# Three-product fp32r projection tiles for q, k, v and conv in a hybrid decoder layer, with the first 16 K pages loaded up front

## The reference

```
p = rmsnorm(h, norm_w) @ w_in           # 9232 columns: conv q/k/v, z, a, b, q_b, k_b, v_b, two gates
q, k, v = silu(causal_conv(qkv))        # gated delta rule, chunked, 8 heads of 128
o_a = gdn_scan(...)
z = q_b @ k_b * SCALE + bias            # stick-breaking attention on the prompt
# the 8 sampled tokens: the same against 2048 cached keys and values each
kp = cache_k[page_table]; vp = cache_v[page_table]      # 16 pages of 128 rows, 8 heads x 128
z = einsum('bqhd,bkhd->bhqk', q, kp)
m = sigmoid(gate_a) * (o_a @ w_pa) + sigmoid(gate_b) * (o_b @ w_pb)
h = h + m @ w_o;  h = h + (silu(gate) * up) @ w_ffn_out;  y = rmsnorm(h)
```

## Time and profile before

| what | value |
|---|---|
| three runs | 1638.34, 1641.56 (median), 1643.76 us |
| profiled execution | 1639.83 us, its span 1638.1 us |
| mean granted TensorE clock in it | 0.934 of full speed |
| busy | PE 1496.4 us (91%), DVE 751.4, ACT 503.7, POOL 139.4 |

### The profile page before, as it was taken

How to read it: one execution, slowest core, us unless ns; L and a number is a source line. 1 busy time by engine, 2 the same in 40 slices (tenths; PEclk the granted TensorE clock), 3 DMA queues, 4 the chain that set the end, 5 groups by cost and what they waited for, 6 DMA issues and landing times.

```text
span 1638.1 us, 26196 instructions
## 1 busy us (share of the span) xinstructions
PE 1496.4 (91%) x9866; PEld 1303.6 (80%) x9866; DVE 751.4 (46%) x2955; ACT 503.7 (31%) x725; POOL 139.4 (9%) x228
## 2 busy tenths in 40 slices
PE   6999897778999988896999899999889999999997
PEld 4777775556778778895877677889879999999996
DVE  2018745997986855654133221225343333332223
ACT  3011015652574322342122434222233222322122
POOL 0000001111221033210041000000000000000000
PEclk9999898998999997787799899999899999999998
DMA  3249873667774420001979998964122333332321
GB/s 108 64 120 329 263 240 137 202 193 242 235 231 138 123 75 7 8 1 30 284 255 329 341 313 262 324 206 143 52 65 78 95 98 91 90 91 81 97 81 52
DMA packets 238754, 252.98 MB, mean 154 GB/s; under 512 B 22361, under 2 KB 197603, under 8 KB 238597
## 3 DMA queue, kind: packets, MB, share of 16 engines
q1 hardware_dynamic: 238629, 251.31, 48.1%
HBM read 236.18 MB, written 15.29 MB: 154 GB/s over the span
## 4 chain that ended last, share of the span: by engine, by line
PE 73%; DVE 13%; DMA 4%; ACT 4%; issue 2%; POOL 2%; SPq 1%; POOLq 0%; DVEq 0%; ACTq 0%
PE ps L883 39%; PE ps L864 14%; DVE kring L1811 5%; PE ps L912 4%; DMA kring<-in_cache_k 3%; PE ps L965 2%; PE ps L848 2%; PE ps L1244 1%; PE ps L1144 1%; PE ps L976 1%; PE ps L938 1%; PE ps L1263 1%; PE ps L1161 1%; PE ps L1134 1%; PE ps L836 1%
## 5 line engine op out<-in xcount | busy, mean ns | idle before, releaser
L864 PE MATMUL ps<-xn,wring 128*128 128x268 f32 (+2 forms) x1568 | 363.7, 393 | 5.3 <-DVE xn L1794 4.4
L864 PEld LDWEIGHTS ps<-xn,wring 128*128 128x128 f32 (+1 forms) x1568 | 296.8, 190 | 69.6 <-issue 13.2
L1811 DVE CUSTOM_DVE_ANT_0 kring<-kring,qv 128x128 f32<-128x128 f32 x1024 | 231.9, 294 | 46.4 <-DMA kring<-in_cache_k 46.2
L1403 ACT ACTIVATE R<-ps 128x520 f32<-128x520 f32 (+1 forms) x86 | 52.4, 610 | 450.8 <-PE ps L864 237.6
L494 DVE TENSOR_TENSOR wring_split<-wring,vring_split 128x1024 fp32r<-128x1024 f32 (+1 forms) x76 | 90.8, 1195 | 204.0 <-ACT vring_split L487 204.0
L883 PE MATMUL ps<-xn_split,vring_split 128*128 128x260 f32 x704 | 142.2, 283 | 7.6 <-DVE obT_split L508 7.6
L883 PE MATMUL ps<-obT_split,vring_split 128*128 128x260 f32 x704 | 142.8, 284 | 0.0
L883 PE MATMUL ps<-xn_split,wring_split 128*128 128x260 f32 x704 | 142.0, 283 | 0.0
L487 ACT ACTIVATE vring_split<-wring 128x1024 fp32r<-128x1024 f32 (+1 forms) x76 | 78.5, 1034 | 171.0 <-DMA wring<-in_w_ffn_out 102.9
L883 PEld LDWEIGHTS ps<-xn_split,vring_split 128*128 128x128 f32 x704 | 109.1, 190 | 8.2 <-issue 7.6
L883 PE MATMUL ps<-R_split,vring_split 128*128 128x260 f32 x592 | 111.3, 285 | 2.3 <-DVE rows_split L508 2.3
(11 more groups left out here) (371 smaller groups left out, 2223.7 us busy)
## 6 DMA issues: line engine op xcount, KB each, us to landing
kring<-in_cache_k SPq DMA_DIRECT2D x128, 512.0 KB, 4.7
wring<-in_w_in SPq DMA_DIRECT2D x72, 512.0 KB, 5.2
vring<-in_cache_v SPq DMA_DIRECT2D x64, 512.0 KB, 5.5
kring<-in_cache_v SPq DMA_DIRECT2D x64, 512.0 KB, 5.4
wring<-in_w_ffn_in SPq DMA_DIRECT2D x44, 512.0 KB, 3.8
wring<-in_w_ffn_out SPq DMA_DIRECT2D x16, 512.0 KB, 3.8
qv<-qdram SPq DMA_DIRECT2D x8, 512.0 KB, 5.7
out_rec_sample<-R SPq DMA_DIRECT2D x4, 1024.0 KB, 10.1
```

The costliest lines, as they stand in the source:

```text
L864: last = mm(ps[0:m, 2 * (t % 2) + i, 0:n], w_block(p, kk), src[:, k, a + i * n:a + i * n + n], start=(k == 0), stop=(k == n_k - 1))
L1403: go(halves(dst[:, first_token(t):TOKENS]), pair(t, m), func).then_inc(act_read, 1)
L1811: m = v.tensor_tensor_reduce(kh, kh, qbc[:, b % 2, h * P:h * P + P], 1.0, 0.0, ALU.mult, ALU.add, dz[:, b % 4, p * H + h:p * H + h + 1])
```

## The change

- Tiles 0 to 48 are computed by `tile_split` as well; `tile` is gone. The parts of `xn` are made straight after the norm: `gate_lo` stands between the normalising instructions on DVE, `gate_hi` on ACT, and tile 0 waits for them block by block. They are gone from the delta-rule chunks. The parts cover all 536 tokens now.
- The high weight parts lie in places that `high_slot` names. `SPLIT_AT` says in which tile's turn ACT and DVE split which weights: one tile ahead up to turn 10 and from turn 43, two tiles ahead between. DVE writes the low parts of tiles 0 to 26, POOL those of tiles 27 to 48 (`pool_lo`).
- The 16 K pages of sampled token 0 are loaded right behind the first four weight tiles, into 16 places at once. Its query row is spread without memory: DVE makes a diagonal matrix of one head (`diagonal`), PE multiplies it by ones (`spread_head`), ACT copies the result (`row_of`), and DVE then takes that head of all 16 pages (`first_head`). This lies in the turns of the q tiles and of the first two k tiles.
- The K pages left are dealt out anew: 18 and 16 in s = 0 and 1 (32 and 16 before), 44 in the attention (40), 34 in the conv tiles (40). The ring has 6 slots up to the end of the attention, 4 after. SP puts the weight load ahead of the K pages of its turn in s = 2 to 4.
- The attention's output goes to `qbT` instead of `obT`; two buffers that POOL clears move from the second conv tile to the 23rd.

```diff
+SPLIT_AT = {}
+for _p in range(2, T_Z):
+    SPLIT_AT.setdefault(min(t for t in range(T_Z) if t + split_lead(t) >= _p), []).append(_p)
...
-K_PLAN = [((0, q), 8) for q in range(4)] + [((1, q), 4) for q in range(4)]
-K_PLAN += [(("att", i), 3 - i % 2) for i in range(2 * H)]
+K_PLAN = list(zip([(0, q) for q in range(4)], (4, 5, 5, 4))) + [((1, q), 4) for q in range(4)]
+K_PLAN += [(("att", i), 3 - (i % 4 == 3)) for i in range(2 * H)]
...
+        def pool_lo(pool, p):
+            pool.wait_ge(w_lo, p)
+            pool.wait_ge(w_hi, p + 1)
+            nc.gpsimd.tensor_tensor(fr(wlo[:, p % RING, :]), wring[:, p % RING, :], w_high(p), ALU.subtract)\
+                .then_inc(w_lo, 1)
...
+            def spread_head(h):
+                pe.wait_ge(q_diag, h + 1)
+                if h >= 2:
+                    pe.wait_ge(q_row, h - 1)
+                mm(ps[:, 6 + h % 2, 0:P], ones[:, :], diag[h % 2][:, :], start=True, stop=True).then_inc(q_mm, 1)
...
             for t in range(T_SEG):
-                tile(t, xn, t == 0)
-            wait_read(pe, T_SEG - 1)
+                tile_split(t, n_hi, n_lo, None if t else 0, first_token(t), g_lo)
+                if t == 2:
+                    decay_rows()
+                    pe.wait_ge(cb_c, 2)
+                if t >= 2:
+                    spread_head(t - 2)
...
+            def row_of(h):
+                act.wait_ge(q_mm, h + 1)
+                nc.scalar.copy(qbc[:, 0, h * P:h * P + P], ps[:, 6 + h % 2, 0:P]).then_inc(q_row, 1)
...
             for n in range(KT):
+                splits(T_Q + n)
                 read_tile(T_Q + n, qbT[:, n, :])
-            decays()
+                if n >= 2:
+                    row_of(n - 2)
+                if n == 4:
+                    decays()
...
+            def first_head(h):
+                dve.wait_ge(q_row, h + 1)
+                for p in range(PAGES):
+                    kh = k_view(p)[:, h * P:h * P + P]
+                    m = v.tensor_tensor_reduce(kh, kh, qbc[:, 0, h * P:h * P + P], 1.0, 0.0, ALU.mult,
+                                               ALU.add, dz[:, 0, p * H + h:p * H + h + 1])
+                    if h == H - 1:
+                        m.then_inc(k_used, 1)
...
+            for h in range(H):
+                splits(T_Q + h)
+                diagonal(h)
+                if h == 0:
+                    dve.wait_ge(k_first, 16 * PAGES)
+                if h >= 1:
+                    first_head(h - 1)
+                if h == 2:
+                    decays()
+                if h == 5:
+                    log_decays()
+            splits(T_SEG)
+            first_head(H - 1)
+            scale_scores(0)
+            splits(T_SEG + 1)
...
             for n in range(NQKV):
+                for p in SPLIT_AT.get(T_SEG + 2 * KT + n, ()):
+                    pool_lo(pool, p)
                 pool.wait_ge(act_read, READ_COUNT[T_SEG + 2 * KT + n])
```

More of the change, by code:

```diff
@@ L78 @@
 TILES = T_FO + KT
-FIRST_SPLIT = T_SEG + 5 * KT
+T_Z = T_SEG + 5 * KT
 def reader(t):
@@ L137, with k_slot, k_use, k_before @@
     _n += _count
+K_LATE = PAGES + sum(_count for _key, _count in K_PLAN if _key[0] in (0, 1, "att"))
+def k_slot(n):
+    if n < PAGES:
+        return n
+    return (n - PAGES) % 6 if n < K_LATE else (n - K_LATE) % RING
+def k_use(n):
+    return sum(k_slot(m) == k_slot(n) for m in range(PAGES, n + 1))
+def k_before(n):
+    return max((m for m in range(n) if k_slot(m) == k_slot(n)), default=None)
 K_ISSUE = {}
@@ L411, in build @@
         w_in_slot = [sem(f"w_in_slot{i}") for i in range(RING)]
-        k_in = [sem(f"k_in{i}") for i in range(RING)]
+        k_in = [sem(f"k_in{i}") for i in range(6)]
+        k_first, q_diag, q_mm, q_row = sem("k_first"), sem("q_diag"), sem("q_mm"), sem("q_row")
         v_in = [[sem(f"v_in{r}_{i}") for i in range(RING)] for r in range(2)]
@@ L627, in _ @@
             sp.dma_start(io["conv_sample"][:, 0:2, :], io["state_conv3"][:, 1:3, :]).then_inc(c_out, 16)
-            for p in range(T_SEG + 3):
+            for p in range(RING):
                 w_load(sp, p)
@@ L651, in spread_q @@
                 sp.dma_start(qbc[:, b % 2, :], qdram[b:b + 1, :].to_broadcast([P, D])).then_inc(qb_in[b % 2], 16)
+            for p in range(PAGES):
+                if p == PAGES - 2:
+                    sp.wait_ge(par_t, 2)
+                page_into(k_view(p), 0, p).then_inc(k_first, 16)
+            for p in range(RING, T_SEG + 3):
+                w_load(sp, p)
+            for i in range(2):
+                for b, p in K_ISSUE[-1, KT - 2 + i]:
+                    k_page(b, p)
             def v_quad(n):
@@ L1635, in _ @@
                         exp_decays()
+                    if t == 11:
+                        act.wait_ge(k_used, PAGES)
+                    if s == 2 and j == 5:
+                        act.wait_ge(k_used, K_LATE)
+                    if s == 3 and j == 0:
+                        act.wait_ge(ob_out, 16)
+                    if s < 5:
+                        splits(t)
                     if (s, j) in SOFT_AT:
@@ L2199, in _ @@
                 for q in range(4):
+                    t0 = T_SEG + s * KT + 2 * q
+                    if (s, q) != (0, 0):
+                        splits(t0)
                     if (s, q) in SP_AT:
@@ L2208, in _ @@
                         conv((s - 2) * KT + 2 * q - 2)
+                        if s < 4:
+                            splits(t0 + 1)
                         conv((s - 2) * KT + 2 * q - 1)
-                    for b, p in K_PAGES.get((s, q), []):
+                    pages = K_PAGES.get((s, q), [])
+                    for i, (b, p) in enumerate(pages):
+                        if i == 2 and s < 2 and (s, q) != (0, 0):
+                            splits(t0 + 1)
                         k_page(b, p)
+                    if (s, q) == (2, 0) or s == 4:
+                        splits(t0 + 1)
                     if (s, q) == (3, 3):
```

207 lines of the change are left out of this document (114 added, 93 removed).

## The result

| | median of the runs | lowest to highest |
|---|---|---|
| before | 1641.76 us | 1638.34 to 1643.76 (4 runs) |
| changed | 1691.49 us | 1690.44 to 1693.89 (4 runs) |

The ratio is 1.0307, with a 95% interval of 1.0286 to 1.0328: the change makes the kernel 50 us slower, where 28 were forecast. The profiled execution of the changed kernel has a span of 1690.7 us at a mean granted clock of 0.912 (before 1638.1 at 0.934).

The account below looks back on a forecast made before the run. PE was taken as full in the q, v and conv stages, neither PE nor DVE in the attention, the chunks as chains between engines. 30 + 2 + 0 - 4 = +28 us gave 1670 in median terms, range 1641 to 1692.

Parts of the forecast that it names:

- the eight waits: Q stage: PE idles 5.6 us ahead of each of tiles 4 to 11, plus 2.0 each for a slower clock.
- The rival in which the clock holds: Waits in q, k and v cost no clock speed: all nine clock terms go, -18, giving 1652; chance 0.14.
- The stop ahead of tile 12: In k: tile 12's low part comes 17.6 us after tile 11's start; 9.6 of waiting remain, plus 2.0 for the clock.
- the rest of k and v: Tiles 12 to 24 run at 5.95 us each, 77.4, with 2.2 of small products: 79.6 us.
- The first sum: Q, k and v stages together: 231.4 us against 201.3 before, so +30, ends +12 and +42.
- the 8.98 idle is gone in it: End of k: PE's 8.98 us idle, waiting for the first token's scores, would disappear.
- the attention: Four more pages in the attention cost +2 us, ends 0 and +3.2.
- the conv tiles: Conv stage: DVE, held by POOL's subtractions, keeps it at 208 us; change 0, ends -30 and +16.
- The hold as such: Conv stage: POOL's 22 subtractions keep DVE still for 32 us, or 48 if each takes 2.5 us.
- The case with 2.5 us: Conv stage: POOL subtractions of 2.5 us, all felt, +16: 1686; or late pages, +12; chance 0.15, up to 1700.
- GpSimd beside VectorE: Conv stage: both engines work side by side, so it gains 30 us: total 1637.5, given 1620 to 1652; chance 0.15.
- the chunks: Chunks: eight subtractions leave DVE, the first three directly ahead of a product the chain needs: -4 us, ends 0 and -5.

Follow-up runs that it names:

- e_fill: The changed kernel with 40 unused matmuls ahead of each of tiles 4 to 11, so PE is not idle in the waits: 1677.19 us.
- e_order: The changed kernel with DVE writing the next tile's low weight part ahead of a head's sixteen pages in the q stage: 1635.44 us.
- e_late: e_order with VectorE, not GpSimd, writing the conv tiles' low parts, behind a turn's two convolutions and first page: 1624.58 us.
- e_conv32: The changed kernel with its 24 conv tiles as one fp32 product again, leaving out the activations' low part there: 1670.33 us.
- e_best2: e_t12b and e_late joined: reordered q stage, earlier weight loads, VectorE writing the conv low parts behind its convolutions: 1618.69 us.
- e_t12b: e_order with weight loads of tiles 12 to 18 moved earlier and DVE's low parts at most one tile earlier: 1628.95 us.
- e_best: e_late with weight loads of tiles 12 to 18 ahead of pages and DVE subtracting for them earlier: 1641.02 us.

## Why the prediction was off

The spans differ by 52.6 us, 24.6 more than the forecast of 28. Of these 24.6 the conv tiles have 13.8, q, k and v 9.5, the chunks 5.1 and the attention 0.5; the gap ahead of the attention gives back 2.5 and the rest of the kernel 1.8. The time came 22 us above the forecast of 1670, at the upper edge of its range.

**Right: the eight waits.** Their number, place, cause and length (5.38 to 6.03 but for the last of 4.04, 5.6 forecast) and the clock behind them (1.9 each by e_fill, 2.0 forecast) came as worked out, and e_order takes them away with one reordering. The rival in which the clock holds is refuted. The stop ahead of tile 12 came too: 18.3 us from the start of tile 11 to tile 12, 17.6 forecast. That this fits so well is in part luck: between SP's write of the query row and its read 5.6 us passed (172.83 to 178.47), not 1.8, while DVE could use the row 3.5 us later, not 6.4.

**Too small: the rest of k and v.** The first sum said 30, and the end of v came 39.5 later. Up to the start of tile 12 (190.14) the sum is short by 2.4. From there to the end of v it is 88.6 us, where I had 2.0 + 79.6 = 81.6. The step that failed is "the 8.98 idle is gone in it": 3.86 us of that stop for the first token's scores stayed, and 1.9 of slow clock behind it (tile 16 takes 7.87 us, not 5.95). Behind the stop ahead of tile 12 the clock cost 2.8, not 2.0 (tile 12 takes 8.73). Against that, PE waited only 1.5 us, not 4.0, between v and the attention, which I had not looked at.

**Right: the attention**, +2.5 for +2.

**Mis-sized: the conv tiles.** This is the largest miss. The term was DVE's work plus its idle time, 193 + 15 = 208, so 0 against before. Measured, it is 200.1 + 22.1 = 222.2, so +13.8. That DVE sets the pace there is seen in who waits for it. ACT's tile reads, which free the banks for PE, waited 6.7 us for DVE's convolutions before, 2 times, and wait 38.6 now, 7 times:

```profile
ACT R L1403 <- DVE R L1895: 6.7, 2, 4.0
...
ACT R L1471 <- DVE R L2002: 38.6, 7, 12.8
```

About half of the 13.8, the 7.1 us of work, comes from GpSimd's instruction: 2.40 us where I took the 1.9 of two instructions with broadcast operands, though I had bounded it at 2.5. The hold as such: e_order's page, convolution and inversion instructions on DVE took 93.2 + 63.9 + 12.7 + 12.7 = 182.5 us, the same in e_late 66.4 + 54.8 + 10.7 + 10.7 = 142.6. That is 40 us for 22 instructions, between my 32 and 48. The other half is idle time of DVE (7.7 us ahead of the inversion's products, 5.1 for a page, 5.2 for ACT), of which I let too little stay; what makes that idle time was not tried. The half-size estimate from GPSIMD Engine Reference of the Trainium skill, section 3, 2.25 us, was nearer to the measured 2.40 than the row that I chose. The case with 2.5 us, which I gave 1686 and a chance of 0.15 together with late pages, comes nearest to what happened: +13.8 for its +16 in the conv stage, and the stop at the end of k can be counted to the late pages.

**Refuted: GpSimd beside VectorE.** e_late against e_order: take the 22 instructions off GpSimd, and DVE needs less time for all it had (186.5 us busy in the stage against 201.4), though it does them itself. Yet three products gain nothing in that stage even then: it lasts some 212 us against 209.5 with fp32 tiles. DVE has 29 us of subtractions to do in it; that these alone hold it there was not tested.

**Wrong in kind: the chunks**, -4 forecast, nothing won (115.5 us before and after). A subtraction straight ahead of the needed product in DVE's queue looked like a cost; but DVE waited for PE ahead of that product anyway, and PE was busy beside it.

The sum of what was measured, 39.5 - 2.5 (gap) + 2.5 + 13.8 + 1.1 (chunks) - 1.8 (rest) = 52.6, is the difference of the two spans.

## What to carry to other kernels

Where an engine has both bulk work and a short step that the next tile needs, the short step goes ahead of the bulk work: one such swap was worth 56 us here, more than the whole change cost. Where a step moves to another engine or earlier in a queue, ask what it will wait for there and who stands behind it; the same 43 us of waiting cost next to nothing on GpSimd (PE waited 3.2 us for it) and more than the hold on VectorE. An instruction straight ahead of a needed one is on the path only if what it delays is what the next engine lacks last.

## What the hardware showed that I had not expected

The chunks ran at two speeds. The same 745 matmuls between the same two GpSimd instructions took 115.6 us in e_order and 106.7 in e_late, at granted clocks of 0.81 and 0.89 (the third column from the right), with equal busy times on DVE, ACT and POOL:

```profile
641.70:757.30 115.60, 98.69 (x745) 94.16 (x743) 64.80 (x161) 36.11 (x76) 26.24 (x25) 0.81 0.03 6
```

```profile
630.60:737.30 106.70, 89.82 (x745) 85.38 (x743) 64.76 (x161) 36.11 (x76) 26.18 (x24) 0.89 0.04 6
```

The kernel before and the changed one had 0.81, e_conv32 had 0.87 and 110.6 us, e_best2 0.89 and 106.7. So the 20 us between the profiled executions of e_order and e_late at the mark behind the chunks are 10 of the conv stage, 9 of this clock and 1 more. In both, the engines' programs are the same in that stretch, and what sets the level in it was not found.

Nor is it shown that the level belongs to a version: each has one profile, and much speaks for the single execution. The profiled executions of e_late and e_best2, with 0.89, are the shortest of their kernels' four runs. Those of e_t12b (1635.90) and e_best (1644.03), with 115.5 us for the stretch, are the longest of four and the second longest of ten, and e_best has the conv stage of e_late. The medians say the same: e_late's is 10.9 us below e_order's, and the conv stage alone accounts for 9.6. So the 9 us are not put down to an edit here, and only marks ahead of the chunks compare versions closely.
